# Attention of a hybrid decoder layer: softmax reciprocals spread over the partitions through DRAM, values copied out of PSUM before they are scaled

## The reference

```python
# latent attention, block i of 8
sc = jnp.einsum('bqhd,bkhd->bhqk', qi, k) * scale          # masked to kpos <= qpos
pr = jax.nn.softmax(sc, axis=-1).astype(v.dtype)
out_i = jnp.einsum('bhqk,bkhd->bqhd', pr, v)
# windowed attention: softmax over [scores of two blocks, sink], then the same product
...
y = jnp.concatenate([y_ssd, y_mla, y_swa], axis=-1) @ w_out[l]
x = x + g1 * y
```

## Time and profile before

| | |
|---|---|
| median of 3 runs | 2294.43 us (2293.14 to 2296.67) |
| profiled execution | 2295.75 us |
| its span, first to last instruction | 2294.0 us |
| mean granted clock of TensorE | 0.991 |
| PE busy | 2250.7 us (98%) |
| DVE busy | 1642.4 us (72%) |
| ACT busy | 1104.0 us (48%) |
| POOL busy | 974.6 us (42%) |
| DMA | 317.13 MB, mean 138 GB/s |

### The profile page before, as it was taken

How to read it: one execution, slowest core, us unless ns; L and a number is a source line. 1 busy time by engine, 2 the same in 40 slices (tenths; PEclk the granted TensorE clock), 3 DMA queues, 4 the chain that set the end, 5 groups by cost and what they waited for, 6 DMA issues and landing times.

```text
span 2294.0 us, 31143 instructions
## 1 busy us (share of the span) xinstructions
PE 2250.7 (98%) x11377; PEld 1844.6 (80%) x11377; DVE 1642.4 (72%) x2280; ACT 1104.0 (48%) x1818; POOL 974.6 (42%) x634
## 2 busy tenths in 40 slices
PE   6999999999999999999999999999999999999998
PEld 6887868887788888888878787788878888888887
DVE  7985466458878887778898744762796666667886
ACT  5355557444444444444543464772444444444455
POOL 3222322445988888300002124153399777760000
PEclk7999999999999999999999999999999999999999
DMA  9742220341444443577457222224323333337763
GB/s 331 283 136 69 66 74 20 129 143 43 160 127 140 118 142 106 170 280 252 146 211 249 63 70 62 50 86 132 105 83 97 115 93 117 94 124 272 255 203 115
DMA packets 273606, 317.13 MB, mean 138 GB/s; under 512 B 33869, under 2 KB 188288, under 8 KB 272687
## 3 DMA queue, kind: packets, MB, share of 16 engines
q1 hardware_dynamic: 271663, 312.11, 42.1%
q10 hardware_dynamic: 1072, 2.23, 0.4%
q0 software_dynamic: 720, 0.81, 0.1%
HBM read 248.37 MB, written 62.54 MB: 136 GB/s over the span
## 4 chain that ended last, share of the span: by engine, by line
PE 88%; POOL 4%; DVE 3%; issue 2%; DMA 1%; SPq 1%; ACT 1%; DVEq 0%; POOLq 0%; ACTq 0%
PE bank L1575 30%; PE bank L1135 19%; PE bank L1591 17%; PE bank L1192 7%; PE bank L1464 2%; PE bank L1429 1%; POOL prodLo L1760 1%; PE bank L1347 1%; PE bank L1394 1%; DVE hLo L2232 1%; POOL tLo L1764 1%; SPq L544 1%; PE bank L1396 1%; PE bank L1395 1%; PE bank L1387 1%
## 5 line engine op out<-in xcount | busy, mean ns | idle before, releaser
L1055 POOL TENSOR_TENSOR wLo<-raw,wHi 128x1024 fp32r<-128x1024 f32 x66 | 161.2, 2444 | 407.6 <-ACT wHi L1057 407.6
L1760 POOL TENSOR_TENSOR prodLo<-comb,prodHi 128x512 fp32r<-128x512 f32 x160 | 245.5, 1542 | 110.4 <-ACT prodHi L1097 110.4
L1575 PE MATMUL bank<-tHi,prodHi 128*128 128x512 f32 x640 | 251.2, 393 | 9.7 <-DVE part L2610 4.5
L1575 PE MATMUL bank<-tHi,prodLo 128*128 128x512 f32 x640 | 249.2, 389 | 0.0
L1575 PE MATMUL bank<-tLo,prodHi 128*128 128x512 f32 x640 | 249.1, 389 | 0.0
L1591 PE MATMUL bank<-gateHi,downHi 128*128 128x512 f32 x616 | 240.3, 390 | 0.1
L1591 PE MATMUL bank<-gateHi,downLo 128*128 128x512 f32 x616 | 239.7, 389 | 0.0
L1591 PE MATMUL bank<-gateLo,downHi 128*128 128x512 f32 x616 | 239.7, 389 | 0.0
L1097 ACT ACTIVATE prodHi<-comb 128x512 fp32r<-128x512 f32 x160 | 100.8, 632 | 260.5 <-PE bank L1575 242.7
L2588 DVE SCALAR_TENSOR_TENSOR ub<-bank,ffp,ub 128x1023 f32<-128x1023 f32 x88 | 112.8, 1282 | 103.3 <-ACT ub L2036 101.7
L1575 PE MATMUL bank<-hHi,prodLo 128*128 128x512 f32 x480 | 186.7, 389 | 0.0
(11 more groups left out here) (432 smaller groups left out, 5380.0 us busy)
## 6 DMA issues: line engine op xcount, KB each, us to landing
raw<-in_ffn_w_up_dram SPq DMA_DIRECT2D x88, 512.0 KB, 4.8
gateRaw<-gateOut SPq DMA_DIRECT2D x154, 256.0 KB, 4.2
adaE<-in_ada_w_dram SPq DMA_DIRECT2D x64, 512.0 KB, 6.4
gateOut<-gateSums SPq DMA_DIRECT2D x22, 1024.0 KB, 5.5
raw<-in_w_in_dram SPq DMA_DIRECT2D x34, 512.0 KB, 4.0
downRaw<-in_ffn_w_down_dram SPq DMA_DIRECT2D x66, 256.0 KB, 3.8
raw<-in_w_out_dram SPq DMA_DIRECT2D x28, 512.0 KB, 3.8
downCols<-in_ffn_w_down_dram SPq DMA_DIRECT2D x24, 512.0 KB, 3.6
```

Source lines behind the costliest of these rows:

```text
L1055: eng.tensor_tensor(lo[:], raw[slot][:], fview(hi[:]), ALU.subtract).then_inc(s["split_lo"], 1)
L1575: last = mm(o, w[idx][:, c0], moving(idx, kp, hi), start=kp == 0 and q_ == 0, stop=kp == 3 and q_ == 2)
L1760: pool.tensor_tensor(sLoW[idx][:], product_source(js, idx), fview(sHiW[idx][:]), ALU.subtract).then_inc(s["us_lo"], 1)
```

## The change

`inverse_sums` goes, and with it 16 groups of products in each layer. In its place SP stores the reciprocals of a finished block, as they stand (128 queries x 4 heads, single elements of 4 B), into a DRAM tensor `invOut`, waits for that, and loads them back in two transfers, each spread over 64 partitions (`spread_inverse`, new). `invSum` has four buffers now, in another place, and `attOut` four.

ACT no longer copies inverses; it copies the block's values from PSUM to `attOut` one unit after the block's last (`copy_block`), and PE waits for this copy before it writes the next block's values. DVE multiplies in place in SBUF three units after the last (before: one), ACT makes the high part four units after (before: two), DVE the low part five units after (before: three).

In SP's order 15 of the 16 spreads of a layer stand before the load of pack 22, with the SSD norm's store and spread between them, and the last one between the two loads of `x`. On PE steps 4 and 5 of packs 20 and 21 come last: 3, 6, 7 of pack 20, then 0, 1, 2, 3, 6, 7 of pack 21, then 4, 5 of both.

```diff
@@ SP @@
+            def spread_inverse(n):
+                kind, i = DONE[n]
+                sp.wait_ge(s["sw_r" if kind == "s" else "ml_r"], nth("sw_r" if kind == "s" else "ml_r", i + 1))
+                sp.dma_start(inv_out[n].rearrange("h q -> q h"), stat[kind][:, i % 3, 2, :], allow_slow_non_contiguous=True).then_inc(s["iv_stored"], 16)
+                sp.wait_ge(s["iv_stored"], nth("iv_stored", 16 * (n + 1)))
+                if n >= 4:
+                    banded, latent = settled(n)
+                    sp.wait_ge(s["sw_x"], nth("sw_x", banded))
+                    sp.wait_ge(s["ml_x"], nth("ml_x", latent))
+                for a in range(2):
+                    sp.dma_start(bcs[n % 4][64 * a:64 * a + 64, :].rearrange("p (j q) -> p j q", j=2),
+                                 inv_out[n:n + 1].rearrange("o (j a) q -> a o j q", a=2)[a].to_broadcast([64, 2, P])).then_inc(s["sw_c" if kind == "s" else "ml_c"], 16)
...
                 if n == N_OUT0 + 2:
-                    store_rstd()
-                    spread_rstd()
+                    ended = [u for u in range(NU) if LAST[UNITS[u][0]][UNITS[u][1]] == u]
+                    for d, u in enumerate(ended[:-1]):
+                        if u > TURN_AT and ended[d - 1] <= TURN_AT:
+                            store_rstd()
+                            spread_rstd()
+                        spread_inverse(d)
...
                     sp.dma_start(xT[:, 0:4, :], xtail[:, 0:4, :]).then_inc(s["tail_loaded0"], 16)
+                    spread_inverse(len(DONE) - 1)
@@ PE @@
                 if i and hs[-1] in (1, 3) and (kind == "s" or hs[-1] == 1):
-                    pe.wait_ge(s["sw_x" if kind == "s" else "ml_x"], nth("sw_x" if kind == "s" else "ml_x", i))
+                    pe.wait_ge(s["sw_b" if kind == "s" else "ml_b"], nth("sw_b" if kind == "s" else "ml_b", i))
...
-            def inverse_sums(kind, i):
-                pe.wait_ge(s["sw_r" if kind == "s" else "ml_r"], nth("sw_r" if kind == "s" else "ml_r", i + 1))
-                for h in range(4):
-                    last = mm(att_bank(kind)[64 * (h % 2):64 * (h % 2) + 64, 256 + (h // 2) * P:256 + (h // 2 + 1) * P],
-                              stat[kind][:, i % 3, 2, h:h + 1].to_broadcast([P, 64]), ident[:], start=True, stop=True)
-                last.then_inc(s["sw_b" if kind == "s" else "ml_b"], 1)
...
-            out_steps(0, (3, 6, 7, 4, 5))
-            out_steps(1, (0, 1, 2, 3, 6, 7, 4, 5))
+            out_steps(0, (3, 6, 7))
+            out_steps(1, (0, 1, 2, 3, 6, 7))
+            out_steps(0, (4, 5))
+            out_steps(1, (4, 5))
@@ ACT @@
-                A(bcs[n % 2][:], half(3, 0 if kind == "s" else 1)[:, 256:512], ACT.Copy).then_inc(s["sw_c" if kind == "s" else "ml_c"], 1)
+                A(ytk[n % 4][:], half(3, 0 if kind == "s" else 1)[:, 0:256], ACT.Copy).then_inc(s["sw_b" if kind == "s" else "ml_b"], 1)
...
-                    for w, todo in ((u - 1, copy_inverse), (u - 2, att_hi)):
+                    for w, todo in ((u - 1, copy_block), (u - 4, att_hi)):
@@ DVE @@
-                dve.tensor_tensor(ytk[n % 2][:], half(3, 0 if kind == "s" else 1)[:, 0:256], bcs[n % 2][:], ALU.mult).then_inc(s["sw_x" if kind == "s" else "ml_x"], 1)
+                dve.wait_ge(s["sw_c" if kind == "s" else "ml_c"], nth("sw_c" if kind == "s" else "ml_c", 32 * (i + 1)))
+                dve.wait_ge(s["sw_b" if kind == "s" else "ml_b"], nth("sw_b" if kind == "s" else "ml_b", i + 1))
+                dve.tensor_tensor(ytk[n % 4][:], ytk[n % 4][:], bcs[n % 4][:], ALU.mult).then_inc(s["sw_x" if kind == "s" else "ml_x"], 1)
...
-                for w, todo in ((u, inverse_of), (u - 1, att_scaled), (u - 3, att_lo)):
+                for w, todo in ((u, inverse_of), (u - 3, att_scaled), (u - 5, att_lo)):
```

More of the change, by code:

```diff
@@ L189, with settled @@
 N_PV = sum(PAIR_END)
+def settled(n):
+    return N_INV_S[n - 3], n - 3 - N_INV_S[n - 3]
 PER_LAYER = {
@@ L318, in build @@
     stat = {k: place(f"stat_{k}", [P, 3, 3, 4], F32, R[13] + 8320 + 192 * n) for n, k in enumerate("sm")}
-    bcs = [place(f"invSum{i}", [P, 256], F32, R[11] + K * i) for i in range(2)]
-    ytk = [place(f"attOut{i}", [P, 256], F32, R[11] + 2 * K + K * i) for i in range(2)]
+    bcs = [place(f"invSum{i}", [P, 256], F32, at["f"] + K * i) for i in range(4)]
+    ytk = [place(f"attOut{i}", [P, 256], F32, R[11] + K * i) for i in range(4)]
     spreadA = place("cumSpread", [P, 8, P], F32, E[0])
@@ L403, in build @@
     rstd_out = nc.dram_tensor("rstdOut", [1, 2 * NB, P], F32, kind="Internal").ap()
+    inv_out = nc.dram_tensor("invOut", [len(DONE), 4, P], F32, kind="Internal").ap()
     gate_out = nc.dram_tensor("gateOut", [P, 7, NK, HALF], F32, kind="Internal").ap()
@@ L519, in build @@
         sw_vt sw_vcopied sw_m k_rope un_s un_n un_e un_t un_ca un_cd un_o
[L520 removed]
+        iv_stored sw_r sw_b sw_c sw_x sw_hi sw_lo ml_r ml_b ml_c ml_x ml_hi ml_lo
         cum_stored cum_loaded sd_xe sd_xe0 sd_t sd_c sd_xt sd_xd sd_bt sd_cb sd_seg sd_dec sd_M sd_yd sd_yd_read sd_eb sd_o sd_st sd_y
@@ L1965, in exps, with copy_block @@
                     A(prs[i % 2][:, :, 256], nsink[:], ACT.Copy).then_inc(s["sw_m"], 1)
-            def copy_inverse(kind, i):
-                act.wait_ge(s["sw_b" if kind == "s" else "ml_b"], nth("sw_b" if kind == "s" else "ml_b", i + 1))
+            def copy_block(kind, i):
+                act.wait_ge(s["un_o"], nth("un_o", PV_BY[LAST[kind][i]]))
                 n = N_INV[kind][i]
-                if n >= 2:
-                    act.wait_ge(s["sw_x"], nth("sw_x", N_INV_S[n - 1]))
-                    act.wait_ge(s["ml_x"], nth("ml_x", n - 1 - N_INV_S[n - 1]))
-                A(bcs[n % 2][:], half(3, 0 if kind == "s" else 1)[:, 256:512], ACT.Copy).then_inc(s["sw_c" if kind == "s" else "ml_c"], 1)
+                if n >= 4:
+                    banded, latent = settled(n)
+                    act.wait_ge(s["sw_lo"], nth("sw_lo", banded))
+                    act.wait_ge(s["ml_lo"], nth("ml_lo", latent))
+                A(ytk[n % 4][:], half(3, 0 if kind == "s" else 1)[:, 0:256], ACT.Copy).then_inc(s["sw_b" if kind == "s" else "ml_b"], 1)
             def att_hi(kind, i):
@@ L1977, in att_hi @@
                 dst = sHi if kind == "s" else mHi
-                A(dst[:, :, i * BLK:(i + 1) * BLK], ytk[N_INV[kind][i] % 2][:].rearrange("p (k t) -> p k t", k=2), ACT.Copy).then_inc(s["sw_hi" if kind == "s" else "ml_hi"], 1)
+                A(dst[:, :, i * BLK:(i + 1) * BLK], ytk[N_INV[kind][i] % 4][:].rearrange("p (k t) -> p k t", k=2), ACT.Copy).then_inc(s["sw_hi" if kind == "s" else "ml_hi"], 1)
             exps(0)
-            for u in range(NU + 2):
+            for u in range(NU + 4):
                 def finish():
@@ L2517, in _ @@
             least(1)
-            for u in range(NU + 3):
+            for u in range(NU + 5):
                 if u + 2 < NU:
```

16 lines of the change are left out of this document (3 added, 13 removed).

## The result

The changed kernel takes 2502.16 us (median of 5 runs, 2500.04 to 2502.95), the kernel before 2294.54 us (5 runs, 2293.14 to 2296.67). The ratio is 1.090, with a 95% interval of 1.089 to 1.092: 208 us slower. The prediction of 2296.4 us, range 2284 to 2310, was wrong.

What follows compares the result with a forecast made beforehand. TensorE, 88% of the chain, was taken as the bound. A layer: 8.6 gained - 0.5 lost on ScalarE - 6.8 stand - 2.3 clock = -1.0; two layers 2.0 us longer, 2296.4 us, range 2284 to 2310.

Steps and rivals of the forecast that it cites:

- I take 3.0 for the store: SyncE's store of a finished block's 512 single elements of 4 B takes 3.0 us, between 1.4 and 5.5.
- cover of 7.2 us: In the attention loop, from a block's reciprocal to the third unit's copy end: 7.2 us, against a trip of 6.5.
- second rival: The 4 B store is slow and the loop's cover goes: 2314 with a store of 5.0, 2302 with 4.0; chance 0.24.
- stand: At the end of each layer's attention TensorE stands 6.8 us waiting for pack 21, bounds 2.9 and 13.8.
- (f): ScalarE splits the last block's values before pack 21, then GpSimd makes its low part: 4.3 us from the multiply, 433.6.
- (g): TensorE ends the values at 422.5, does three steps of pack 20 in 4.25 us, wants pack 21 at 426.8.
- (e): At the end of layer 0's attention, the last block's spread takes 0.4 + 2.6 us, until 429.3.
- (d): The last block's reciprocal is stored behind the 2 MB of x, 1.4 us on top, done at 426.3.
- first rival: The stand is short, 3 to 5 us, perhaps without a clock fall: 6 to 10 us faster, 2284 to 2289; chance 0.27.
- all at 5.5: Upper bound with store and spread at 5.5 us: a stand of 13.8, 18 us slower, 2312.7.
- less than 7: Attention values ending less than 7 us a layer earlier, instead of 8, would point to ScalarE or VectorE as bound.
- third rival: ScalarE or VectorE bounds the attention loop, so TensorE gains only half of 8.6 us a layer: 2304; chance 0.10.

Runs made afterwards that it cites:

- first kernel with whole rows: Changed kernel storing 128 pieces of 16 B, spreading whole 2 KB rows, ScalarE splitting pack 21 ahead of both last blocks' output: 2296.95 us, ratio 1.001.

## Why the prediction was wrong

**The step that failed** is "I take 3.0 for the store", with its bounds of 1.4 and 5.5. Alone on the queue the store is 9.7 us, in the kernel 9.3. The nearest row that I took, the weights of 32 KB in 512 pieces, and the row of 5.5 are both loads; no store of small neighbouring pieces stood in the trace, and the upper bound was no bound. I had written that the point was a store over 3.7, and had even weighed a rule against the change: the Trainium skill (DMA: Bandwidth & Descriptors, Specifications) says that a transfer below 512 B becomes a read-modify-write. No run shows whether that happens. What they show is that being below 512 B does not by itself make a store slow: pieces of 4 B cost 9.6 or 2.0 us by their distance, 128 pieces of 16 B 1.7, 128 of 128 B 1.4, and 16 rows of 512 B 1.3.

**The loop.** "I cost the loop's waits at 0" became 134.2 us. The cover of 7.2 us was counted from the reciprocal's start (from its end it is 7.0), and it holds for a block alone. Of two blocks that end close together the second also waits for SyncE, which the sum left out; with spaced stores TensorE stands 3.6 of the 5.2 us right behind such a pair, the same one in each layer (1.05 at 389.31, 2.58 at 1519.34). The second rival had the mechanism and the wrong size. With a store of 9.3 its trip is 12.8, 5.6 us over the cover; by its own arithmetic (8 blocks, half of it free) that is 22 us a layer, and with all 16 blocks 90. Measured are 67 of idle TensorE and some 26 of lowered clock. What it missed is that SyncE, which serves one block at a time, is then the bound for every block, one in 12.2 us.

**Were the store alone to blame?** No. With the store at 2.8 to 2.9 us, as I had taken it, the kernel takes 2313.94 us, beyond the range's 2310. Both layers together, in us:

| | forecast | stores 64 B apart | no store | changed |
|---|---|---|---|---|
| products gone | -17.2 | -12.7 | -12.7 | -12.7 |
| idle in the loop | 1.0 | 5.2 | 1.6 | 134.2 |
| stand | 13.6 | 16.4 | 7.5 | 30.0 |
| clock (busy time above 2238.0) | 4.6 | 7.0 | 1.2 | 52.3 |
| sum | 2.0 | 15.9 | -2.4 | 203.8 |
| measured span | | 18.8 | -1.2 | 204.6 |

**The stand.** (f) and (g) held in both kernels: from the multiply to pack 21's first product 4.3 us (4.3), from the end of the values to the need 4.4 (4.25). (e), from the last spread to the multiply (3.0), was 3.3 in the changed kernel, 528.20 to 531.50, but 5.3 and 6.4 with spaced stores; why is open. (d), the last store behind the first 2 MB, was to end 11.2 us after the issue of the 2 MB. With spaced stores it took 10.1 (418.96 to 429.02), in the changed kernel 14.5 (513.72 to 528.20). So the stand of 7.3 us in layer 0 with spaced stores is near my 6.8 because two errors cancel, and layer 1 had 9.1. Without a store it was 3.9 and 3.6, the first rival's 3 to 5. The upper bound was also summed wrongly: with "all at 5.5" step (d) has 3.0, and with 5.5 there it comes out 5 us higher, at 2318.

**The gain.** 256 products went, but they were worth 6.0 us a layer up to the end of the values and not 8.1, and the stage ended 5.0 earlier, where I had allowed a loss of 0.5. By my own sign (less than 7) the third rival, ScalarE or VectorE as the bound, should have been true; only 1.0 of the 3.1 missing is such a wait.

**The clock.** I took 2.3 us a layer behind the stand, and that held. Without a store the granted clock was 0.70 over 432 to 435 and 0.84 over 435 to 440, which is 1.7 us lost, and 3.1 in layer 1; with spaced stores 2.3 (0.65 over 438.5 to 445) and 3.2. What I did not cost is the clock inside the loop: in the changed kernel it was 0.77 over 326 to 519. In the table's row the 4.8 us without a store shrink to 1.2, by the two differences of 1.7 us named with the account.

**The multiply from two SBUF operands.** In the changed kernel it takes 425 ns in the median, at most 2060. I had priced it at 0 on the path, and there the store hides it. In the first kernel with whole rows, which reads every fourth element, it is longer:

```profile
L2511 DVE TENSOR_TENSOR attOut<-attOut,invSum x32: 583/610/2411, 339.7 to 1557.2; 128x256 f32<-128x256 f32 x32
```

(duration in ns, least, median, most). The one of 2060 starts at 1660.90, beside a product of GpSimd at 1660.34 to 1662.68. That GpSimd makes it long is likely but not tried alone, and no run shows what it costs on the path.

**The forecast's time** was met by the kernel without any store, 2296.59 us. That is chance: it took the gain 2.6 us a layer too large and the stand 3.0 too large.

## What to carry over

Before a small on-chip product is replaced by a trip through DRAM, price the store by the layout of its pieces in DRAM: let each partition write what it holds in one piece, 16 B at least, or set pieces 32 B apart, and do the rearranging on the reading side. A number that the trace does not show, on which a cover with 0.7 us to spare rests, is worth more range than the nearest rows give. And when work is taken off the busiest engine just ahead of a hand-over, look at what the next stage is waiting for: here a gain of 5 us a layer ran into a pack that was ready 2.2 us early before. A group's step from start to start (0.54 us) is not what its removal gives back (0.40).

## What the runs showed of the hardware

- A store of 128 x 4 pieces of 4 B, alone on the queue, is 9.6 us when they lie side by side, 3.7 at 8 B, 3.0 at 16 B, 2.1 at 32 B and 2.0 at 64 B; 128 such pieces side by side are still 7.4.
- Such a store moves 2 KB, and yet a load queued behind it lands 12 us after its issue, with a DMA share of 0.05 meanwhile (342 to 349). A low share does not mean that the queue is free.
- A spread of 64 KB in runs of 512 B and one of 128 KB in runs of 2 KB cost about the same, 2.6 to 3.8 and 3.2 to 3.3 us to land.
